# PEER down projection: order of VectorE's and ScalarE's splits of activations and weights in the loop over 64 units

## What is computed

```python
def chunk(args):
    hc, ec, gc = args
    u = peer_u[ec]
    a = jax.nn.gelu(jnp.einsum("ckd,cd->ck", u, hc)) * gc
    vv = peer_v[ec]
    return jnp.einsum("ck,ckd->cd", a, vv)
```

## Time and profile before

| | |
|---|---|
| median of 3 runs | 2862.53 us (2862.51 to 2865.07) |
| profiled execution, its time | 2861.7 us |
| profiled execution, its span | 2859.8 us |
| TensorE busy | 2754.3 us (96%) |
| VectorE busy | 2224.7 us (78%) |
| ScalarE busy | 1459.4 us (51%) |
| mean granted clock of TensorE | 0.986 |

### The profile page before, as it was taken

How to read it: one execution, slowest core, us unless ns; L and a number is a source line. 1 busy time by engine, 2 the same in 40 slices (tenths; PEclk the granted TensorE clock), 3 DMA queues, 4 the chain that set the end, 5 groups by cost and what they waited for, 6 DMA issues and landing times.

```text
span 2859.8 us, 37083 instructions
## 1 busy us (share of the span) xinstructions
PE 2754.3 (96%) x13531; PEld 2317.7 (81%) x13531; DVE 2224.7 (78%) x3019; ACT 1459.4 (51%) x1956; POOL 630.7 (22%) x507
## 2 busy tenths in 40 slices
PE   5989969999999999999999999999999999999998
PEld 4767848888888768777787899999999988888887
DVE  7576658888888863888864899999777668888886
ACT  4344238888888744554543334566666533333332
POOL 0321111111111100000020000334333324444442
PEclk7999979999999999999999999999999999999999
DMA  8754539999999733333343234789988999999995
GB/s 319 238 198 160 184 130 348 372 369 367 359 357 360 290 123 123 103 120 102 128 148 128 97 132 166 285 305 327 342 322 309 321 357 362 353 360 357 364 361 174
DMA packets 201723, 738.01 MB, mean 258 GB/s; under 512 B 24352, under 2 KB 77728, under 8 KB 144960
## 3 DMA queue, kind: packets, MB, share of 16 engines
q1 hardware_dynamic: 124656, 497.12, 48.1%
q0 software_dynamic: 55008, 170.98, 17.0%
q10 hardware_dynamic: 21872, 67.48, 6.1%
HBM read 666.61 MB, written 94.04 MB: 266 GB/s over the span
## 4 chain that ended last, share of the span: by engine, by line
PE 61%; DVE 14%; issue 5%; DMA 3%; ACT 2%; POOL 0%; ACTq 0%; DVEq 0%; SPq 0%; POOLq 0%
PE PS L548 54%; DVE wlo L1950 3%; PE PS L1183 2%; DMA ht<-in_peer_v_dram,IDX 1%; PE PS L861 1%; PE PS L1060 1%; DVE hf L2757 1%; ACT whi L1259 1%; DVE oh L2743 1%; DVE zo L2480 1%; DVE hf L2769 1%; ACT HH L1920 1%; DVE cand L2704 1%; DVE cand L2706 1%; PE PS L1046 1%
## 5 line engine op out<-in xcount | busy, mean ns | idle before, releaser
L1950 DVE TENSOR_TENSOR wlo<-raw,whi 128x2048 fp32r<-128x2048 f32 x392 | 894.4, 2289 | 270.8 <-ACT whi L1259 251.1
L1259 ACT ACTIVATE whi<-raw 128x2048 fp32r<-128x2048 f32 x392 | 751.0, 1917 | 356.3 <-PE PS L548 303.9
L548 PE MATMUL PS<-HH,whi 128*128 128x512 f32 (+1 forms) x2064 | 783.5, 380 | 10.2 <-DVE HL L2003 4.3
L548 PE MATMUL PS<-HH,wlo 128*128 128x512 f32 (+1 forms) x2064 | 750.4, 364 | 0.0
L548 PE MATMUL PS<-HL,whi 128*128 128x512 f32 (+1 forms) x2064 | 750.0, 363 | 0.0
L548 PEld LDWEIGHTS PS<-HH,whi 128*128 128x128 f32 x2064 | 389.2, 189 | 65.0 <-issue 14.5
L548 PEld LDWEIGHTS PS<-HL,whi 128*128 128x128 f32 x2064 | 389.7, 189 | 44.5 <-issue 5.5
L548 PEld LDWEIGHTS PS<-HH,wlo 128*128 128x128 f32 x2064 | 388.6, 188 | 42.9
L548 PE MATMUL PS<-whi,HH 128*128 128x512 f32 x864 | 341.6, 395 | 13.7 <-DVE HL L2801 8.3
L548 PE MATMUL PS<-wlo,HH 128*128 128x512 f32 x864 | 338.0, 391 | 0.0
L548 PE MATMUL PS<-whi,HL 128*128 128x512 f32 x864 | 338.0, 391 | 0.0
(11 more groups left out here) (456 smaller groups left out, 3830.5 us busy)
## 6 DMA issues: line engine op xcount, KB each, us to landing
raw<-in_moe_dram SPq DMA_DIRECT2D x192, 1024.0 KB, 7.3
raw<-in_u_units_dram SPq DMA_DIRECT2D x64, 1024.0 KB, 6.2
raw<-in_v_units_dram SPq DMA_DIRECT2D x64, 1024.0 KB, 8.9
raw<-in_w_in_dram SPq DMA_DIRECT2D x44, 1024.0 KB, 5.2
raw<-in_w_ada_dram SPq DMA_DIRECT2D x24, 1024.0 KB, 6.7
acts_dram<-sS ACTq DMA_DIRECT2D x64, 384.0 KB, 5.8
gates_dram<-XT ACTq DMA_DIRECT2D x24, 1024.0 KB, 8.0
sS<-acts_dram SPq DMA_DIRECT2D x42, 384.0 KB, 6.9
```

The lines of the kernel that those rows point to most:

```text
L548: ins = t.matmul(dst, a, b, start=(first and n == 0), stop=(last and n == 2))
L1259: a.inc(a.e.activation(m.whi[p % HRING][:, :, :], m.raw[RAW_SLOT[load_of(p)]][:, :, :], ACT.Copy), "hi", p)
L1950: v.inc(v.e.tensor_tensor(m.wlo[h][:, :, :], m.raw[RAW_SLOT[load_of(p)]][:, :, :], m.whi[h][:, :, :].bitcast(F32), ALU.subtract), "lo_v", p)
```

## The change

In the loop VectorE gates the activations of unit u+1 before it makes `wlo` of unit u+2, and makes their `HL` behind it; before, both came behind it. ScalarE makes `HH` of unit u+1 before `whi` of unit u+2; before, after it. Everything else stays as it is.

```diff
@@ -1921,9 +1921,9 @@
 
     prepare(0)
     for u in range(64):
-        act_high(a, m, FIRST["v_units"] + u + HRING - 1)
         if u + 1 < 64:
             prepare(u + 1)
+        act_high(a, m, FIRST["v_units"] + u + HRING - 1)
         for n in (2 * u, 2 * u + 1):
             for step in PEER_DOWN[n]:
                 act_gather_step(a, m, step)
@@ -2790,22 +2790,28 @@
     v.wait_ge(f"gate5_out{(N_GATE // 4 - 1) % 2}", N_GATE // 4 - 1)
     v.wait_ge(f"gate5_out{N_GATE // 4 % 2}", N_GATE // 4 - 2)
 
-    def prepare(u):
+    def gated(u):
         i, g, k = u % 3, u // 4, u % 4
         v.wait_ge(f"acts_in{i}", u)
         v.wait_ge(f"gates_in{g % 2}", g)
         sa = bass.AP(m.sA[i], 0, [[2 * TDN, 128], [TDN, 2], [16, NG], [1, 16]])
         v.inc(e.tensor_tensor(sa, sa, bass.AP(m.Gin[g % 2], 32 * k, [[m.GSTR[g % 2], 128], [16, 2], [128, NG], [1, 16]]),
                               ALU.mult), "gated", u)
+
+    def low_half(u):
+        i, k = u % 3, u % 4
         v.wait_ge("ahi", u)
         v.inc(e.tensor_tensor(m.HL[:, 2 * k:2 * k + 2, TD:], m.sA[i][:, :, :],
                               m.HH[:, 2 * k:2 * k + 2, TD:].bitcast(F32), ALU.subtract), "alo", u)
 
-    prepare(0)
+    gated(0)
+    low_half(0)
     for u in range(64):
+        if u + 1 < 64:
+            gated(u + 1)
         dve_low(v, m, FIRST["v_units"] + u + HRING - 1)
         if u + 1 < 64:
-            prepare(u + 1)
+            low_half(u + 1)
         for n in (2 * u, 2 * u + 1):
             for step in PEER_DOWN[n]:
                 dve_gather_step(v, m, step)
```

## The result

| | before | changed |
|---|---|---|
| median, us | 2863.62 (5 runs, 2862.51 to 2865.07) | 2955.86 (5 runs, 2953.27 to 2956.61) |
| profiled execution, span, us | 2859.8 | 2953.2 |

The ratio of changed to before is 1.0319, 95% interval 1.0307 to 1.0330. The change costs 92 us, 3.2%. The forecast was 2956.0.

What follows compares the result with a forecast made beforehand. TensorE was taken to bound the kernel before, busy 502.61 of 508.00 us in the stage's middle. Terms +91.8, +4.5 and -2.4 made +93.9 us on 2861.7 profiled, giving a forecast median of 2956.0 us, range 2948 to 2974.

Steps and rivals of the forecast that it cites:

- Who sets the pace: In the v_units loop, VectorE sets the pace in every turn: 9.58 us with two rows against TensorE's 8.16.
- ring through ScalarE: Each turn, VectorE's gating, then ScalarE's HH and whi, then VectorE's wlo wait in sequence: 3.91 us from gating to wlo.
- Term 1: Loop from wlo of unit 2 to wlo of unit 63: 599.8 us instead of 508.0, +91.8 us.
- rival (3): ScalarE's step from HH to whi costs 0.29 us more per period, 18 us in all: 2974 us; chance 0.12.
- Term 2: Stage entry: wlo of unit 2 waits behind the second gating, whose activations are read from memory: +4.5 us.
- Term 3: Stage end: wlo of unit 63 to the first addition of the sums shortens from 22.35 to 19.9 us: -2.4 us.
- Transfers: In the loop, transfers stay hidden and cost nothing; the DMA share falls from 0.97 to about 0.82.
- rival (1): TensorE's clock falls in the stage because of its stands, up to 68 us on top, 3024 us; chance 0.10.
- second branch of the rival: Clock falls only behind three-row turns; their 2.8 us of TensorE slack takes the whole 2.5 us loss: 2956 us.
- The first branch: Clock loss of 2.5 us in every unit: 1.4 goes into slack, 68 us come on top, 3024 us.
- TensorE's waits: In the stage, TensorE waits for HL in every unit, 1.4 us each, near 95 to 105 us in all.
- Rival (2): VectorE doesn't become the bound in the loop; TensorE's 5.4 us of short waits vanish: 2856 us; chance 0.03.

Runs made afterwards that it cites:

- e2: Changed kernel with VectorE's row steps moved from behind HL to between the gating and wlo; 2857.11 us, ratio 0.9975 to the kernel before.
- e4: Changed kernel with one more ScalarE copy of the gated activations ahead of HH in each turn; 3000.54 us, ratio 1.0474 to the kernel before.
- e5: Kernel of e1 with the same additional ScalarE copy as in e4; 2856.03 us, ratio 0.9975 to the kernel before.
- e1: Kernel before with VectorE's half of the change alone, ScalarE still making whi before HH; 2856.26 us, ratio 0.9971.
- e6: Kernel before with VectorE's gating and HL both moved ahead of wlo, ScalarE still making whi before HH; 2855.60 us, ratio 0.9972.
- e3: Changed kernel with 12 of 256 rows left out, so no turn has three row steps; 2940.47 us, ratio 1.0267 to the kernel before.

## Why the prediction was right, step by step

**Who sets the pace** was right: VectorE, in every turn, by a ring through ScalarE. e2 shows that the ring is the cause (rows under the hand-over, and the loss is gone), e4 and e5 that added time on ScalarE is open in this ring and hidden in the order of e1, and e1 that the other half of the change is harmless.

**Term 1**, forecast +91.8 us, is +90.3 (598.3 against 508.0). The steps came out within 0.02 us: gating to `HH` 1.05 (forecast 1.04), `HH` to `whi` 0.75 (0.75), `whi` to `wlo` 2.10 (2.12), `wlo` to `HL` 2.21, `HL` to row 0.87, and from the last row to the gating 1.20. The period is 9.56 against 9.58. The one value read at a single place, 0.75, held, so rival (3) fell.

**Term 2**, the entry, forecast +4.5 us, is +3.3. TensorE's first matmul of the stage is the fixed point: `wlo` of unit 2 started 0.91 us behind it before (2311.99 to 2312.90) and 4.18 behind it now (2313.16 to 2317.34). VectorE's timeline at the entry:

```profile
2312.10 0.96 DVE L2804 TENSOR_TENSOR HL<-sA,HH 128x768 fp32r<-128x768 f32 x1 [4.04 <-ACT HH L1920]
2313.49 0.96 DVE L2798 TENSOR_TENSOR sS<-sS,XT 128x768 f32<-128x768 f32 x1 [0.43 <-DMA sS<-acts_dram]
2317.34 2.29 DVE L1950 TENSOR_TENSOR wlo<-raw,whi 128x2048 fp32r<-128x2048 f32 x1 [2.89 <-ACT whi L1259]
```

The gating waited only 0.43 us for the activations; it started 1.39 us behind `HL` (2312.10), where I had 2.6. The timeline of SyncE's queue has the issue of that read:

```profile
2309.99 0.33 SPq L3213 DMA_DIRECT2D sS<-acts_dram  x1
```

From 2309.99 to the gating at 2313.49 it took 3.5 us. The mechanism was right; the term that was mis-sized is the read, 4.4 us in the forecast, 3.5 measured. The rest, 0.3 us, is its issue relative to the stage and rounding.

**Term 3**, the end, forecast -2.4 us, is -2.3 (20.02 from `wlo` of unit 63 to the first addition, against 22.35). But the tail behind it was not unchanged, as I had it: from that addition to the end it took 17.5 us against 16.5. The windows view of the tail, first of the changed kernel, then of the kernel before:

```profile
2941.00:2949.00 8.00, 7.49 (x44) 7.52 (x45) 4.25 (x9) 0.85 (x3) 0.00 (x0) 0.63 0.51 146
```

```profile
2848.00:2856.00 8.00, 6.93 (x47) 6.96 (x48) 5.17 (x11) 1.42 (x3) 0.00 (x0) 0.79 0.55 160
```

TensorE's clock is 0.63 here and was 0.79, in the 48 matmuls behind its last long stand (3.7 us now, 4.1 before): they took 8.18 us instead of 7.22. That is the 1.0 us. Nothing ties it to the change: the same 48 took 7.22 us in the profiles of e1 to e4 and 8.52 and 8.27 in e5 and e6, and the stand ahead of them was 4.1 us in e6 as in the kernel before. The profile closes: +1.2 us ahead of the stage (TensorE's first matmul at 2313.16 instead of 2311.99, where the two programs are the same), +3.3, +90.3, -2.3, +1.0 make 93.4 before rounding, the difference of the spans. That the total agrees to half a microsecond is luck: terms 1 and 2 were 2.7 too high together, and 2.2 came from places outside the sum.

**Transfers**, put at nothing, cost nothing: in the loop the changed kernel's waits view shows VectorE waiting for a transfer only in the 0.4 us at the entry, the short waits of the rows are gone, and the DMA share is 0.84 where I had 0.82.

**TensorE's clock**, rival (1), deserves more than the chance I gave it, and would still not have changed the time. The stands of 2.5 us behind three rows did bring the clock down in 7 of 11 units. TensorE's timeline behind the first of them:

```profile
2379.05 0.47 PE L548 MATMUL PS<-whi,HH 128*128 128x512 f32 x1 [2.55 <-DVE HL L2804]
...
2380.67 0.63 PE L548 MATMUL PS<-whi,HH 128*128 128x512 f32 x1
2381.10 0.63 PE L548 MATMUL PS<-wlo,HH 128*128 128x512 f32 x1
...
2383.93 0.39 PE L548 MATMUL PS<-whi,HL 128*128 128x512 f32 x1
```

Eight matmuls are 0.43 apart instead of 0.23, 1.6 us lost, and the next unit then starts without a stand: the unit took 8.16 + 1.6 = 9.8 us, 0.2 more than the 9.56 that VectorE's pace leaves it. The stand after that is shorter by these 0.2 (0.90 us as shown, at 2398.17), and TensorE is back behind VectorE, two periods of 9.56 after 2379.05. That is the second branch of the rival as put down, "its slack would take it all", though it was the slack of the next two units that took it, not the stand of 2.8 ahead; e3 confirms it. The first branch, a fall in every unit, did not come: no unit behind a stand of 1.1 us ran at the lower clock. So of the Trainium skill's remark on short idles ("TensorE: Matmul & The Clock Gate", "A second HAM failure mode: psum-queue depth-cycling") the trace shows the clock going down and up again, 7 times, but no price in the stage's time, since VectorE set the pace there.

**TensorE's waits** were forecast at 95 to 105 us and read 76.8. The stands are there, 598.3 - 61 x 8.16 = 100.5 us, but the view shows less for two reasons: seven units filled them with slow matmuls, and a lost 1.40 us is shown as 1.12 to 1.15, since a matmul's record is 0.39 long while the next may start 0.23 after it (0.16 hidden), and the first starts behind a stand are 0.30 and 0.24 apart (0.1 more). The same effect hid a part of what there was to win. The twelve short waits of the earlier trace rows summed to 5.4 us as shown, but TensorE took 530.8 us from its first matmul of the stage to its last, where 64 x 8.16 = 522.2 would do: 8.6 lost. e1 gained 8 in the medians (5 to 11 by its interval) and 6.0 in the spans, where its profile had 13 matmuls at the lower clock at the entry, 0.2 us each.

**Rival (2)** fell: gating to `wlo` cost 3.90 us, not under 2.49. Its idea, that `HL` no longer waits for `HH`, is true and worth something, but only with ScalarE's order of before (e1) or with the rows under the hand-over (e2).

## What to carry to other kernels

When two engines feed each other in order, write down one turn of each queue as starts and ask what each engine can do while it waits for the other; an instruction of 1.9 us that was free behind other work costs its full time once nothing stands between the request and the wait. Busy shares don't show it: ScalarE was at 27% and each 0.73 us given to it cost 0.73 us a turn. Order cured it here (e1, e2): let the slow helper's instruction that needs nothing from this turn (`whi`) go first, or put independent work between the request and the wait.

## What I had not expected of the hardware

TensorE's clock fell to the lower level behind single stands of 2.5 us, 7 times of 11, with full work before and behind, while the 41 stands of about 1.1 us (0.9 to 1.15 as shown) never did it. In e4 it fell behind 9 of the 35 stands shown as 1.7 to 1.9 us and behind 7 of the 9 shown as 3.3, and the page's mean clock was 0.976, from 0.981. And behind the 2.9 us stand at the entry, the same in all kernels, the clock fell in some profiles (matmuls 0.43 apart from 2311.86 on in e1) and not in others (0.23 apart in the kernel before), so one profile doesn't say whether a stand of that length will cost.
